# Four head pairs' outputs turned by VectorE's 32x32 blocks and GpSimd's transfers instead of TensorE

## What is computed

```python
def block(args):                                  # differential attention
    scores = jnp.einsum('bqhmd,bkhmd->bhmqk', q_blk, k) * scale
    scores = jnp.where(causal, scores, NEG_BIG)
    probs = jax.nn.softmax(scores, axis=-1)
    weights = probs[:, :, 0] - lam * probs[:, :, 1]
    return jnp.einsum('bhqk,bkhe->bqhe', weights, v)
...
o = _rms_norm(o, subln_g) * (1.0 - lambda_init)   # over each head's 128 columns
...
branch = jnp.concatenate([tok_out, cross_out], axis=-1) * jax.nn.silu(gate)
y = branch @ w_out[i]
x = x + _rms_norm(y, post_norm[i])
```

## Time and profile before

| | |
|---|---|
| median of 3 runs | 946.15 us (945.61 to 946.81) |
| profiled execution | 946.67 us, its span 944.9 us |
| busy: TensorE, VectorE, ScalarE, GpSimd | 933.8, 636.3, 503.6, 17.2 us |
| granted TensorE clock over the span | 0.998 of full speed |
| transfers | 188.45 MB, 199 GB/s |

### The profile page before, as it was taken

One profiled execution on the slowest core, in us unless ns is written; L12 is line 12 of the kernel. 1 busy time (PEld: TensorE's weight loads), 2 busy tenths in 40 slices (PEclk: granted clock), 3 DMA queues, 4 the chain that ended last, 5 costly groups with the idle time before them and its releaser, 6 DMA issues.

```text
span 944.9 us, 12669 instructions
## 1 busy us (share of the span) xinstructions
PE 933.8 (99%) x4752; PEld 789.4 (84%) x4752; DVE 636.3 (67%) x834; ACT 503.6 (53%) x801; POOL 17.2 (2%) x41
## 2 busy tenths in 40 slices
PE   9999999999999999999999999999999999999996
PEld 7888888888888888888888888888888888888885
DVE  5878766754565475555595558557787888888555
ACT  6867553344344443444465555447586576675542
POOL 0000200000000000000000003000000000000000
PEclk9999999999999999999999999999999999999999
DMA  9757585766766666676566658565755746745652
GB/s 330 244 164 230 170 258 177 213 198 214 221 188 191 187 193 220 228 240 231 178 234 192 184 151 255 171 208 154 216 176 159 222 146 187 221 145 173 222 197 89
DMA packets 124894, 188.45 MB, mean 199 GB/s; under 512 B 7277, under 2 KB 66989, under 8 KB 124330
## 3 DMA queue, kind: packets, MB, share of 16 engines
q1 hardware_dynamic: 122138, 178.80, 60.9%
q10 hardware_dynamic: 1680, 6.85, 2.1%
q0 software_dynamic: 1024, 2.10, 0.9%
HBM read 178.82 MB, written 2.10 MB: 191 GB/s over the span
## 4 chain that ended last, share of the span: by engine, by line
PE 88%; DVE 5%; ACT 2%; DMA 2%; issue 2%; SPq 0%; DVEq 0%; POOL 0%; ACTq 0%; POOLq 0%
PE psum L480 19%; PE psum L481 19%; PE psum L482 19%; PE psum L419 17%; PE psum L420 9%; DVE lo_ring L1037 2%; DMA stage_area<-in_mem_dram 1%; PE psum L499 1%; ACT hi_ring L720 1%; DMA layer_area<-layer_area 1%; ACT layer_area L1001 1%; PE psum L661 1%; DMA raw_ring<-in_w_in_dram 0%; ACT stage_area L810 0%; DVE layer_area L1463 0%
## 5 line engine op out<-in xcount | busy, mean ns | idle before, releaser
L1037 DVE TENSOR_TENSOR lo_ring<-raw_ring,hi_ring 128x1024 fp32r<-128x1024 f32 x318 | 385.6, 1222 | 249.0 <-ACT hi_ring L720 248.4
L720 ACT ACTIVATE hi_ring<-raw_ring 128x1024 fp32r<-128x1024 f32 x318 | 335.4, 1061 | 363.0 <-PE psum L482 253.0
L419 PE MATMUL psum<-hT_split,hi_ring 128*128 128x512 f32 x832 | 292.9, 397 | 0.4 <-DVE lo_ring L1037 0.4
L420 PE MATMUL psum<-hT_split,lo_ring 128*128 128x256 f32 x832 | 232.1, 279 | 0.0
L419 PEld LDWEIGHTS psum<-hT_split,hi_ring 128*128 128x128 f32 x832 | 156.1, 188 | 38.8 <-issue 2.0
L480 PE MATMUL psum<-hi_ring,hT_split 128*128 128x512 f32 x480 | 187.0, 390 | 0.4 <-DVE lo_ring L1037 0.4
L481 PE MATMUL psum<-lo_ring,hT_split 128*128 128x512 f32 x480 | 186.8, 389 | 0.0
L482 PE MATMUL psum<-hi_ring,hT_split 128*128 128x512 f32 x480 | 186.8, 389 | 0.0
L420 PEld LDWEIGHTS psum<-hT_split,lo_ring 128*128 128x128 f32 x832 | 156.8, 188 | 0.1
L480 PEld LDWEIGHTS psum<-hi_ring,hT_split 128*128 128x128 f32 x480 | 90.1, 188 | 19.3 <-issue 0.7
L482 PEld LDWEIGHTS psum<-hi_ring,hT_split 128*128 128x128 f32 x480 | 90.1, 188 | 18.9
(11 more groups left out here) (227 smaller groups left out, 754.4 us busy)
## 6 DMA issues: line engine op xcount, KB each, us to landing
raw_ring<-in_w_in_dram SPq DMA_DIRECT2D x224, 512.0 KB, 3.9
raw_ring<-in_w_out_dram SPq DMA_DIRECT2D x64, 512.0 KB, 4.1
raw_ring<-in_w_kv_mem_dram SPq DMA_DIRECT2D x30, 512.0 KB, 4.3
layer_area<-layer_area SPq DMA_DIRECT2D x48, 64.0 KB, 3.7
x_residual<-in_conv_w_dram ACTq DMA_DIRECT2D x3, 768.0 KB, 6.4
stage_area<-in_mem_dram SPq DMA_DIRECT2D x8, 256.0 KB, 6.6
x_residual<-in_x_dram SPq DMA_DIRECT2D x2, 1024.0 KB, 8.6
layer_area<-in_post_norm_dram ACTq DMA_DIRECT2D x2, 1024.0 KB, 6.2
```

What stands on the lines that cost most here:

```text
L419: mm(o, hi[:, k, P * c:P * (c + 1)], X[:, kt, :], start=kt == 0, stop=False)
L420: last = mm(o[:, SEQ:], lo[:, k, P * c:P * (c + 1)], X[:, kt, 0:SEQ], start=False, stop=kt == KT - 1)
L720: run(whi[:, slot, :], raw[:, slot, :], ACT.Copy).then_inc(hi_ready, 1)
L1037: V_.tensor_tensor(wlo[:, slot, :], raw[:, slot, :], whi[:, slot, :].bitcast(f32), SUB)\
```

## The change

For the outputs of pairs 0 to 3, TensorE's transposes are gone. After the normalising, in the same step 3 of the query group, VectorE turns 32x32 blocks into a freed tile (`out_blocks`); GpSimd issues 16 transfers of 32 partitions by 128 words that move the blocks to `oT`; and VectorE takes them from there (`out_moved`) at the end of the gate group, after the combining and ahead of the activation. `out_take` stays for pairs 4 and 5. TensorE's value products wait for the turned blocks, because they are followed by the overwriting of the normalised outputs. In layer 0 the block turns of the memory weights move from the last column group's step 2 to step 1 of the first mixer row group.

```diff
+    vm_flat = vm.rearrange("p m e -> p (m e)")
+    o_blocks = vm_flat[:, 0:512].rearrange("p (b r g) -> p b r g", b=4, g=4)
+    oT = vm_flat[:, 512:1024].rearrange("p (a r g) -> p a r g", a=4, g=4)
...
-        for l in range(DEPTH):
+        def cross_move(l):
...
+        cross_move(0)
+        cross_move(1)
+        for p in range(PAIRS - 2):
+            pool.wait_ge(o_blocks_turned, p + 1)
+            for a, b in QUADRANTS:
+                nc.gpsimd.dma_start(oT[32 * b:32 * b + 32, a], o_blocks[32 * a:32 * a + 32, b]).then_inc(o_blocks_moved, 16)
...
-        def diff_values(p):
+        def diff_values(p, first=False):
             pe.wait_ge(wt_ready, p * 16 + 16)
+            if not first:
+                pe.wait_ge(o_blocks_turned, p)
...
-        def diff_out_turn(p, exps=None):
+        def diff_out_turn(p):
             pe.wait_ge(on_ready, p + 1)
-            if exps is not None:
-                pe.wait_ge(exp_done, exps)
+            pe.wait_ge(exp_done, PAIRS * 8)
...
-                in_gate[1] = lambda: diff_values(p - 1)
-            if not first and not second:
-                in_keys[3] = lambda: diff_out_turn(p - 2, p * 8)
+                in_gate[1] = lambda: diff_values(p - 1, second)
...
         column_group(G_XG0 + 1, 5, U_XG0 + B_UNITS, 0, val0,
-                     at={2: lambda: cross_blocks(0), 3: lambda: cross_vm_low(0)})
+                     at={3: lambda: cross_vm_low(0)})
...
-            row_group(u, at={5: lambda: branch_low(j - 1)} if j else {})
+            row_group(u, at={5: lambda: branch_low(j - 1)} if j else {1: lambda: cross_blocks(0)})
...
+        def out_blocks(p):
+            dve.wait_ge(on_ready, p + 1)
+            V_.transpose(o_blocks.rearrange("p b r g -> p g b r"), o_sb.rearrange("p g (b r) -> p g b r", b=4))\
+              .then_inc(o_blocks_turned, 1)
+
+        def out_moved(st, p, parity):
+            dve.wait_ge(o_blocks_moved, p * 256 + 256)
+            rows_, gate = (v.rearrange("p c (t q) -> p (c t) q", t=TT) for v in (br1, sgate[parity]))
+            V_.scalar_tensor_tensor(rows_, oT.rearrange("p a r g -> p g (a r)"), subg, gate, MULT, MULT).then_inc(o_taken, 1)
+            dve.wait_ge(o_taken, p + 2)
+            split_branch(st, br1, bass.ds(p * 2, 2), in_order=True)
...
+            def norm_and_turn():
+                out_norm(st, p - 2, parity)
+                out_blocks(p - 2)
...
-                in_query[3] = lambda: out_norm(st, p - 2, parity)
-                in_gate[1] = lambda: out_take(st, p - 2, parity)
+                in_query[3] = norm_and_turn
             column_group(G, c, u, s, two(qT), at=in_query)
             column_group(G + 1, c + 1, u + B_UNITS, 1 - s, two(kT))
             column_group(G + 2, c + 2, u + 2 * B_UNITS, s, val1, at=in_gate)
+            if not first and not second:
+                out_moved(st, p - 2, parity)
             dve.wait_ge(bank_free, G + 3)
             st.did(silu_twice(p + (MIXES + 3), tanh1, val1, sgate[parity]))
```

More of the change, by code:

```diff
@@ L243, in build @@
     u_shifted, taps_loaded = sem("u_shifted"), [sem(f"conv_taps_loaded{j}") for j in range(MIXES)]
+    o_blocks_turned, o_blocks_moved = sem("o_blocks_turned"), sem("o_blocks_moved")
     b_ready, b_turned, b_hi = sem("branch_rows_ready"), sem("branch_rows_turned"), sem("branch_hi")
@@ L688, in last_values @@
         def last_values():
-            diff_out_turn(PAIRS - 2, PAIRS * 8)
-            diff_values(PAIRS - 1)
+            diff_out_turn(PAIRS - 2)
+            diff_values(PAIRS - 1, True)
         for g in range(4):
@@ L1431, in out_norm @@
               .then_inc(on_ready, 1)
+        def out_blocks(p):
[8 more added lines that the diff above has]
+            split_branch(st, br1, bass.ds(p * 2, 2), in_order=True)
         def out_take(st, p, parity):
-            dve.wait_ge(n_done, p + 1)
+            dve.wait_ge(n_done, p - (PAIRS - 3))
             V_.scalar_tensor_tensor(br1, two(ps[:, 7, :]), subg, sgate[parity], MULT, MULT).then_inc(o_taken, 1)
```

## The result

The changed kernel takes a median of 958.44 us (957.95 to 960.22, four runs), the kernel before 946.25 us beside it (945.61 to 946.81, four runs). The ratio is 1.0134, with a 95% interval of 1.0122 to 1.0146: slower by 12.2 us by the medians, 12.7 by the ratio. The direction was forecast; the size, 953.8 us, was 4.6 us short. The time lies on the upper edge of the range, 958.5: the median just inside, and 1.0134 times the 946.15 us that the sum started from, 958.8, just outside. The profiled execution took 960.22 us, its span is 958.4.

A forecast was written before the change was run, and what follows sets the result against it. TensorE, busy 99% of the span, was taken as the bound. First-pair loss 2.39 us plus 4.75 over three periods gave 7.14, or 8.2 with one late transfer, on 946.15: forecast 953.8 us, range 950.5 to 958.5.

The forecast's parts named there:

- Transposes off TensorE: Before the last key unit: four times 0.36 us, 1.44 at most, worth nothing unless the low part comes no later.
- Block turns in front of the low part: On VectorE before the last key unit: turn of 0.86 us delays the low part 0.91 us; first pair loses 0.71.
- Taking at the end of the gate group: On VectorE, 0.88 us: TensorE stands 1.68 us before the score products, and the first pair's loss reaches 2.39 us.
- The cycle from there: Between score products: period of 38.88 us; three take 116.64 against 111.89, so 4.75 us lost.
- the stride's price: Turn and taking at every fourth word: 0.86 and 0.88 us, from a stride-of-three row 1.27 times as long.
- GpSimd's transfers: Sixteen a pair, landing 12.6 us after the turn; hidden by some 7 us before the taking.
- Value products' wait: TensorE's new wait before the value products, for turns done more than a unit before: nothing.
- Layer 0: Moved block turns there: transfers land by 131.8, ScalarE takes them at 132.76; cost nothing, 1 us to spare.
- The gaining case: Rival: VectorE's operations hidden and `o_taken` in time, four pairs save 0.36 us each: 944.7 us; 6%.
- Only the turns: Rival: only the block turns cost, the wait on `o_taken` being hidden; 2.1 us, 948.3 us; 5%.
- The free stride: Rival: the stride of four costs nothing, turn 0.678 and taking 0.69 us: 951.8 us; 20%.
- Crowding: Rival: GpSimd's transfers delay weights and half swaps, 1.07 us in each pair: 957.6 us; 14% together with strides twice as long.

The follow-up runs named there:

- kernel 7: Changed kernel with the outputs' reciprocal root moved early to query step 2, ahead of the softmax weights, and the taking in gate step 1: 945.40 us, 0.9988.
- kernel 8: As kernel 7, but with the taking one step later, in step 2 of the gate group: 945.34 us, 0.9990.
- kernel 12: As kernel 7, but with layer 0 left as in the kernel before: 944.05 us, 0.9975.
- kernel 3: Kernel before with only the four block turns added behind the normalising, their result unused; transposes and taking stay: 950.08 us, 1.0034.
- kernel 4: Changed kernel with the turn moved behind the last key unit's low part, to key step 0; taking stays at the gate group's end: 957.36 us, 1.0104.
- kernel 9: As kernel 7, with the root early, but the taking left at the end of the gate group: 956.45 us, 1.0111.
- kernel 6: Changed kernel with the taking put back to step 1 of the gate group, the turn staying ahead of the low part: 957.43 us, 1.0122.
- Kernel 11: Kernel before with nothing but layer 0's block turns moved: 946.54 us, 1.0001.
- kernel 10: Changed kernel with contiguous blocks: the turn writes 32 words in a row, the taking becomes four operations of 128x128: 957.23 us, 1.0121.
- kernel 2: Kernel before with only GpSimd's 64 transfers added, their result unused: 947.07 us, 1.0006.
- kernel 1: Changed kernel without TensorE's wait on the taking (`o_taken`) before the score products: 959.95 us, 1.0149.
- kernel 5: Changed kernel with fourteen transposes of the identity, computing nothing, ahead of three of TensorE's four waits on the taking: 959.47 us, 1.0143.

## Where the prediction was right, and the two terms that failed

*Transposes off TensorE*, worth nothing: right. With the low part late, TensorE started the last key unit 0.97 us after it could have (696.11). Only kernels 7, 8 and 12, where VectorE has room, get the transposes' time back.

*Block turns in front of the low part*: right in place, short in size. Kernel 3 shows it by itself, 3.6 us; in the changed kernel, where the taking stands in the same cycle, moving it away gains 1.1 (kernel 4). The turn took 1.12 us for the 0.86 that I took; the bound of twice a contiguous turn, 1.36, held it.

*Taking at the end of the gate group*: right in place. TensorE waited there four times, and kernel 9 against 7 gives the place alone 11 us: 7.3 of waits, 1.6 to 2.0 of clock behind one of them, and the rest not taken apart. The step was priced at a wait of 1.68 us and a loss of 2.39 us in the first pair; measured were 2.81 us and 3.68 (40.56 between score products, 36.88 before). The taking took 1.13 us for 0.88, and the keys' half swap came 0.83 us late. The prediction had a late transfer, but of 1.07 us in another pair.

*The cycle from there*: right. With turn and taking at their measured times the period is 38.88 + 0.26 + 0.25 = 39.39 us; the one period with full clock behind its start, from 758.71 to 798.02, is 39.31. That it is so close is partly luck: TensorE's two stretches took 18.74 and 18.56 us for the 18.26, and its waits were 0.23 and 1.78 us for 0.94 and 1.93.

*What failed*: two terms of the sum. The first is the stride's price. I took 0.86 and 0.88 us from the row of a stride of three, 1.27 times as long, where four words cost 1.57 to 1.63 times. That is 0.51 us in the first pair and 0.43 in each of three periods (39.31 for 38.88), 1.8 us. The second is a term that I put at nothing: I had TensorE stand and then go on at full clock. The profile shows half the clock behind three of four waits. The other two periods are 41.44 and 40.27 us, 2.1 and 1.0 above 39.31, 3.1 us. The late half swap of the first pair is the remaining 0.8. With the forecast 7.1 these make 12.8 us, which is what the trace has; it has to come out, since I split the measured gaps that way. Nor was it right that nothing of the change follows behind the last wait: the third low stretch lies there, and 1.5 us with it.

Other numbers bear the clock's share out. TensorE's low stretches cover 6.0, 3.4 and 3.4 us of its work; half of that is 6.4 us, less 1.44 for the transposes 5.0, an estimate, and its busy time grew by 4.7. In kernel 9 one gap of three begins at half clock and is 1.6 to 2.0 us longer than its neighbours. So the clock's share is shown within about a microsecond; what makes it fall behind one wait and not behind another is open.

*GpSimd's transfers* hidden: right at this place, by the rows: VectorE never waits for them. My 12.6 us from turn to landing measured 11.9 to 13.0 in kernels 6 and 7, and in kernel 6 VectorE stood for it. *Value products' wait*: none is in the trace. *Layer 0*: landing was forecast for 131.8 with 1 us to spare; it came 1.2 us later, ScalarE waited 0.48 us, until 133.01, and TensorE never. Kernel 11 shows it to be nothing.

*The rivals.* The gaining case isn't reached by this change, though it can be by another order: kernel 12 is at 944.05, beside the 944.7 that the transposes alone would give. It hung on the room that VectorE has in the query steps, which I had not looked for; the idle of 1.88 us before the softmax weights is in the trace of before too, at 687.77. Only the turns: nearest to it is kernel 3, which measured 950.08 for 948.3, with the transposes still in it. The free stride falls by the groups of kernel 10: 712 ns contiguous, 1118 with it. The Trainium skill ("SBUF — State Buffer", Door 1: The DMA port swizzle, the note on cachelines) had up to four fp32 words free of charge; these rows don't agree. For the write kernel 10 shows it with the layout alone changed; for the read there is only the 1130 against 692 ns of another operation. What its note ties to a cost, each access on a line of its own, is what a stride of four words does, so the trace agrees with the mechanism and not with that bound. Crowding as I had it, 1.07 us in each of four pairs, falls: the changed kernel has one late half swap, of 0.83 us, and kernel 2 loses nothing. A smaller part of it may be in that 0.83.

## What to carry to other kernels

Work taken from the busiest engine gains only if the engine that takes it over has room in the same steps: sum up that engine's work between two places where they wait for each other, and look for its idle time in the rows before you choose a place. If a wait is removed and the time stays, look where it stands now, as in kernels 1, 4 and 6; what must shrink is the cycle. Transfers that are fine late aren't for free early: know their landing time before moving what reads them.

## What the runs showed of the hardware

A stride of four f32 words costs VectorE 1.57 times in the writing of a block turn (1118 against 712 ns). A product that reads one operand at it takes 1130 ns, 1.63 times the 692 ns of a plain product; the two aren't the same operation.

TensorE's granted clock fell to half (1.2 of 2.4 GHz) for 3.4 to 6.8 us behind a standing of 1.8 to 2.8 us, in a stream that is otherwise 98% busy. A gap that began so was 1.0 to 2.1 us longer. It doesn't fall every time, but behind 12 of the 23 standings of 1.7 us or more in the traces of these kernels: not behind 1.88 us at 758.71 in the changed kernel, nor behind 2.90 us in kernel 5, and behind only one of the four of 1.78 to 1.95 us in kernel 9. What decides it is open.

Sixteen small transfers issued by GpSimd take 7.8 us to issue and 11.9 to 13.0 us until VectorE has the last (kernels 6 and 7), with 4 to 5 us of it behind the last issue. Sixty-four of them beside the weights cost no time that shows (kernel 2), but in that trace VectorE waited three times, up to 0.7 us, for a half swap, and once for 0.25 us in the trace without them.
